# A decoder trunk on one core: convolution taps through PSUM, and the spatial branch's scale and offset behind its product

## The reference, cut to what is computed

```python
def conv_sgu_mixer(x, w_in, conv_w, conv_b, conv_ln_g, conv_ln_b,
                   sgu_ln_g, sgu_ln_b, w_spatial, b_spatial, w_out):
    h = x @ w_in                                   # 1024 -> 2048
    a_val, a_gate, z = h[..., :512], h[..., 512:1024], h[..., 1024:]
    a = a_val * jax.nn.sigmoid(a_gate)
    a = causal_depthwise_conv(a, conv_w) + conv_b  # 31 taps, 512 channels
    a = jax.nn.silu(layer_norm(a, conv_ln_g, conv_ln_b))
    z = jax.nn.gelu(z, approximate=False)
    u, v = z[..., :512], z[..., 512:]
    v = layer_norm(v, sgu_ln_g, sgu_ln_b).reshape(B, 4, 128, 8, 64)
    sv = jnp.einsum('hts,bnshc->bnthc', w_spatial * causal, v) + b_spatial.T[None, None, :, :, None]
    g = u * sv.reshape(B, S, 512)
    return jnp.concatenate([a, g], axis=-1) @ w_out
```

## Time and profile before

| | us |
|---|---|
| median of 3 runs | 1517.16 |
| lowest and highest | 1514.57, 1518.96 |
| the profiled execution, its own time | 1517.05 |
| its span, first to last instruction | 1515.2 |
| PE busy (matmul) | 1420.8, 94% of the span |
| DVE busy | 582.7, 38% |
| ACT busy | 494.0, 33% |
| POOL busy | 656.6, 43% |
| mean granted TensorE clock | 0.971 of full |

### The profile page before, as it was taken

One profiled execution on the slowest core, in us unless ns is written; L12 is line 12 of the kernel. 1 busy time (PEld: TensorE's weight loads), 2 busy tenths in 40 slices (PEclk: granted clock), 3 DMA queues, 4 the chain that ended last, 5 costly groups with the idle time before them and its releaser, 6 DMA issues.

```text
span 1515.2 us, 17072 instructions
## 1 busy us (share of the span) xinstructions
PE 1420.8 (94%) x6631; PEld 1194.2 (79%) x6631; DVE 582.7 (38%) x761; ACT 494.0 (33%) x741; POOL 656.6 (43%) x297
## 2 busy tenths in 40 slices
PE   8981699999999998899999999999998999999997
PEld 7760478888888886788889888889878888888885
DVE  4999754111114004667643566643243111110004
ACT  4442354222222124233333333342343222222112
POOL 4982345444444445333344233334244444444442
PEclk9995699999999999899999999999999999999999
DMA  9220123333332322223232222233122333333221
GB/s 266 73 84 0 61 65 98 97 97 97 97 127 97 97 87 67 69 87 96 84 97 84 70 84 83 80 95 104 42 70 86 95 98 96 97 125 97 97 70 56
DMA packets 175551, 135.27 MB, mean 89 GB/s; under 512 B 4317, under 2 KB 157673, under 8 KB 175496
## 3 DMA queue, kind: packets, MB, share of 16 engines
q1 hardware_dynamic: 175496, 134.50, 29.6%
HBM read 132.39 MB, written 2.10 MB: 89 GB/s over the span
## 4 chain that ended last, share of the span: by engine, by line
PE 83%; DVE 12%; ACT 2%; SPq 1%; issue 1%; POOL 0%; DMA 0%; DVEq 0%
PE pq L540 11%; PE pq L542 11%; PE pq L541 11%; DVE acc L1326 7%; PE ps L540 5%; PE ps L541 5%; PE ps L542 5%; PE pq L562 3%; PE pq L563 3%; PE pq L564 3%; PE ps L564 3%; PE ps L562 3%; PE ps L563 3%; PE pq L844 3%; PE pq L846 2%; PE pq L845 2%
## 5 line engine op out<-in xcount | busy, mean ns | idle before, releaser
L474 POOL TENSOR_TENSOR w_lo<-w_stage,w_hi 128x1024 fp32r<-128x1024 f32 x236 | 573.1, 2433 | 766.0 <-ACT w_hi L934 765.8
L540 PE MATMUL pq<-xt_hi,w_hi 128*128 128x512 f32 (+1 forms) x888 | 339.8, 383 | 8.4 <-DVE xt_lo L1223 5.7
L541 PE MATMUL pq<-xt_lo,w_hi 128*128 128x512 f32 (+1 forms) x888 | 336.3, 379 | 0.0
L542 PE MATMUL pq<-xt_hi,w_lo 128*128 128x512 f32 (+1 forms) x888 | 336.1, 379 | 0.0
L934 ACT ACTIVATE w_hi<-w_stage 128x1024 fp32r<-128x1024 f32 x236 | 245.9, 1053 | 269.0 <-PE ps L564 191.9
L540 PEld LDWEIGHTS pq<-xt_hi,w_hi 128*128 128x128 f32 x888 | 169.5, 191 | 40.3 <-DVE xt_lo L1223 6.4
L542 PEld LDWEIGHTS pq<-xt_hi,w_lo 128*128 128x128 f32 x888 | 169.5, 191 | 30.8
L541 PEld LDWEIGHTS pq<-xt_lo,w_hi 128*128 128x128 f32 x888 | 169.6, 191 | 29.7
L1491 DVE TENSOR_TENSOR hidden<-ps,hidden 128x512 f32<-128x512 f32 x44 | 30.4, 692 | 371.0 <-PE ps L542 371.0
L540 PE MATMUL ps<-xt_hi,w_hi 128*128 128x512 f32 (+1 forms) x368 | 139.9, 380 | 0.0
L541 PE MATMUL ps<-xt_lo,w_hi 128*128 128x512 f32 (+1 forms) x368 | 139.8, 380 | 0.0
(11 more groups left out here) (229 smaller groups left out, 2017.5 us busy)
## 6 DMA issues: line engine op xcount, KB each, us to landing
w_stage<-in_od_w_qkv_dram SPq DMA_DIRECT2D x72, 512.0 KB, 3.8
w_stage<-in_ffn_w_gate_dram SPq DMA_DIRECT2D x44, 512.0 KB, 3.8
w_stage<-in_ffn_w_up_dram SPq DMA_DIRECT2D x44, 512.0 KB, 3.8
w_stage<-in_ffn_w_down_dram SPq DMA_DIRECT2D x44, 512.0 KB, 3.3
w_stage<-in_ev_w_in_dram SPq DMA_DIRECT2D x16, 512.0 KB, 6.3
w_stage<-in_ev_w_out_dram SPq DMA_DIRECT2D x8, 512.0 KB, 3.3
w_stage<-in_od_w_out_dram SPq DMA_DIRECT2D x8, 512.0 KB, 3.3
x_res<-in_x_dram SPq DMA_DIRECT2D x4, 512.0 KB, 6.4
```

The costliest lines, as they stand in the source:

```text
L474: pool.tensor_tensor(w_lo[slab % RING][:, :], w_stage[slab % RING][:, :], w_hi[slab % RING][:, :].bitcast(F32), ALU.subtract).then_inc(w_l ...
L540: pe.matmul(ps[bank][:, at], hi[:, k, :], xt_hi[:, k, at], start=(k == 0), stop=False)
L541: pe.matmul(ps[bank][:, at], hi[:, k, :], xt_lo[:, k, at], start=False, stop=False)
L542: last = pe.matmul(ps[bank][:, at], lo[:, k, :], xt_hi[:, k, at], start=False, stop=(k == KD - 1))
```

## The change

- Of the taps, DVE now has 10 of chunk 0 and 26 of chunk 1, so 98 in all, and ACT with POOL 26, two behind each of slabs 5 to 17.
- DVE's running sums lie in PSUM, bank 6 for chunks 0 and 2, bank 7 for chunks 1 and 3; only a chunk's last DVE tap writes `acc`.
- The spatial product is taken over the value norm without its gain and offset. The gain multiplies behind the product, in the gating instruction. The offset becomes part of `b_sp`: PE sums the masked spatial weights with ones (`sum_spatial`, 8 small matmuls behind slab 3), DVE scales the four offset columns and folds them in with four instructions of 128 x 128. The two value-norm passes on DVE are replaced by one small instruction there and four ACT instructions of 128 x 512.
- The v tiles lie in banks 4, 5, 0, 1 and u in 2, 3, 0, 1, with the waits that this needs. The mean over channels goes to bank 2 and behind the first three spatial pairs.
- The taps are interleaved otherwise: after gate 3 come 24 taps, the four statistics together, 8 taps, the small scale instructions, and the last 32.
- SP: gain and offset are rows of `par_rows` (20 rows instead of 12 turned by PE), the two broadcasts `sgu_g` and `sgu_b` go, `b_sp` comes in two transfers instead of eight, slab 4 is loaded ahead of the spatial weights, the constant table `cst` behind them, and slabs 5 to 7 ahead of the norm's parameters.

The diff, cut:

```diff
-        dve_taps = (8, 22)
+        dve_taps = (10, 26)
         pool_taps = [(c, w) for c in range(2) for w in range(dve_taps[c], CONV_WIDTH)]
         chunk_taps = [CONV_WIDTH - n for n in dve_taps]
-        after_slab = {5: 3, 6: 3, 7: 3, 8: 3, 9: 3, 10: 3, 11: 3, 12: 2, 13: 2, 14: 2, 15: 5}
+        after_slab = dict.fromkeys(range(5, 18), 2)
+        v_banks = (4, 5, 0, 1)
+        u_banks = (2, 3, 0, 1)
+        CONV_B, CONV_G, CONV_O, SGU_G, SGU_B = (CC * CONV_WIDTH + n * CC for n in range(5))
...
-            sp.dma_start(cst[:, :], const_in).then_inc(cst_loaded, 16)
             sp.dma_start(par_rows[0:CONV_WIDTH, 0:CONV_CH], ev_conv_w[0]).then_inc(par_loaded, 16)
-            for n, src in enumerate((ev_conv_b, ev_conv_ln_g, ev_conv_ln_b)):
+            for n, src in enumerate((ev_conv_b, ev_conv_ln_g, ev_conv_ln_b, ev_sgu_ln_g, ev_sgu_ln_b)):
                 sp.dma_start(par_rows[4 * n:4 * n + 4, CONV_CH:CONV_CH + P],
                              src[0].rearrange("(c p) -> c p", p=P)).then_inc(par_loaded, 16)
+            load(RING)
             sp.dma_start(wsp_raw[:, :, :], ev_w_spatial[0].rearrange("h t s -> t h s")).then_inc(wsp_loaded, 16)
-            sp.dma_start(sgu_g[:, :], ev_sgu_ln_g.partition_broadcast(P)).then_inc(sgu_loaded, 16)
-            sp.dma_start(sgu_b[:, :], ev_sgu_ln_b.partition_broadcast(P)).then_inc(sgu_loaded, 16)
-            for h in range(SGU_GROUPS):
-                half = (h % 2) * GROUP_CH
-                sp.dma_start(b_sp[half:half + GROUP_CH, h // 2, :],
-                             ev_b_spatial[0, h:h + 1, :].partition_broadcast(GROUP_CH)).then_inc(sgu_loaded, 16)
+            sp.dma_start(cst[:, :], const_in).then_inc(cst_loaded, 16)
+            load(RING + 1)
+            for half in range(2):
+                rows = ev_b_spatial[0].rearrange("(c two) t -> two c t", two=2)[half:half + 1]
+                sp.dma_start(b_sp[half * GROUP_CH:(half + 1) * GROUP_CH, :, :], rows.broadcast_to([GROUP_CH, CC, P])
+                             ).then_inc(sgu_loaded, 16)
+            for slab in range(RING + 2, RING + 4):
+                load(slab)
             load_ln(0, 0, 0)
-            for slab in range(RING, S_UP0):
+            for slab in range(RING + 4, S_UP0):
...
+            def sum_spatial():
+
+                pe.wait_ge(ones_set, 1)
+                pe.wait_ge(wsp_set, 2)
+                for h in range(SGU_GROUPS):
+                    half = (h % 2) * GROUP_CH
+                    last = pe.matmul(ps[5][half:half + GROUP_CH, h // 2 * P:(h // 2 + 1) * P], ones[:, 0:GROUP_CH],
+                                     wsp_t[:, h, :], start=True, stop=True)
+                last.then_inc(offset_summed, 1)
 
             pe.wait_ge(xt_set, 2 * TILES)
 
@@ -612,15 +628,19 @@
                     columns(slab + j, 2 * (c % 2) + j, (2 if c + j == 0 else 0, TILES)).then_inc(w_used, 1)
                 if c == 0:
                     turn_parameters()
+                if c == 1:
+                    sum_spatial()
...
-            pe.wait_ge(wsp_set, 2)
+            pe.wait_ge(offset_set, 1)
             for s in range(4):
                 slab = S_IN + 8 + s
                 slab_ready(slab)
                 for i in range(TILES):
+                    if s == 0 and i == 2:
+                        pe.wait_ge(a_set, 3)
                     for k in range(2):
-                        last = tokens(slab, 512 * k, 512, 4 + i, xt_hi[:, 2 * s + k, :], xt_lo[:, 2 * s + k, :],
+                        last = tokens(slab, 512 * k, 512, v_banks[i], xt_hi[:, 2 * s + k, :], xt_lo[:, 2 * s + k, :],
...
-                if c % 2 == 0:
-                    pe.wait_ge(a_set, 3 + c // 2)
-                columns(slab, c).then_inc(w_used, 1)
-
-            pe.wait_ge(ones_set, 1)
-            pe.wait_ge(v_gelu, TILES)
-            for c, (which, count) in enumerate(((tap_added, chunk_taps[0]), (tap_added, len(pool_taps)),
-                                                (acc_set, 1), (acc_set, 2))):
-                pe.wait_ge(which, count)
-                last = pe.matmul(ps[7][:, :], ones[:, :], acc[:, c, :], start=(c == 0), stop=(c == CC - 1))
-            last.then_inc(mean_done, 1)
+                if c == 0:
+                    pe.wait_ge(a_set, 4)
+                if c >= 2:
+                    pe.wait_ge(v_gelu, c + 1)
+                columns(slab, u_banks[c]).then_inc(w_used, 1)
 
             def spatial(pair):
                 for n in range(TILES):
@@ -651,8 +665,18 @@
                 last.then_inc(sv_done, 1)
 
             pe.wait_ge(v_set, TILES)
+            pe.wait_ge(sum_begun, 2)
             for pair in range(CC - 1):
+                if pair == CC - 2:
+                    pe.wait_ge(acc_set, 1)
                 spatial(pair)
+            for c, (which, count) in enumerate(((tap_added, chunk_taps[0]), (tap_added, len(pool_taps)),
+                                                (acc_set, 1), (acc_set, 2))):
+                pe.wait_ge(which, count)
+                if c == 0:
+                    pe.wait_ge(u_set, 1)
+                last = pe.matmul(ps[2][:, :], ones[:, :], acc[:, c, :], start=(c == 0), stop=(c == CC - 1))
+            last.then_inc(mean_done, 1)
...
             act.wait_ge(v_var, TILES)
             act.activation(std[:, 0:TILES], mean_var[:, :, 1], ACT.Sqrt, bias=eps[:, 0:1]).then_inc(v_std, 1)
             multiply_taps(15)
+            act.wait_ge(v_scale, 1)
+            for i in range(TILES):
+                act.activation(v_tok[:, i, :], v_tok[:, i, :], ACT.Identity, bias=shift[:, i:i + 1],
+                               scale=rstd[:, i:i + 1]).then_inc(v_set, 1)
             for c in range(CC):
                 act.wait_ge(w_used, S_IN + 12 + c + 1)
-                act.activation(u_t[:, c, :], ps[c][:, :], ACT.Gelu).then_inc(u_set, 1)
-                split_high(16 + c)
+                act.activation(u_t[:, c, :], ps[u_banks[c]][:, :], ACT.Gelu).then_inc(u_set, 1)
+                split_and_taps(16 + c)
...
+                    part = ps[6 + c % 2][:, :]
+                    last = w == (dve_taps[c] if c < 2 else CONV_WIDTH) - 1
                     if w == 0:
-                        ins = dve.tensor_scalar(acc[:, c, :], src, weight, bias, ALU.mult, ALU.add)
+                        ins = dve.tensor_scalar(part, src, weight, bias, ALU.mult, ALU.add)
                     else:
                         link.wait(self_tap[c])
-                        ins = dve.scalar_tensor_tensor(out=acc[:, c, :], in0=src, scalar=weight, in1=acc[:, c, :],
-                                                       op0=ALU.mult, op1=ALU.add)
-                    if c < 2 and w == dve_taps[c] - 1:
-                        ins.then_inc(sum_begun, 1)
-                    elif w == CONV_WIDTH - 1:
-                        ins.then_inc(acc_set, 1)
+                        ins = dve.scalar_tensor_tensor(out=acc[:, c, :] if last else part, in0=src, scalar=weight,
+                                                       in1=part, op0=ALU.mult, op1=ALU.add)
+                    if last:
+                        ins.then_inc(sum_begun if c < 2 else acc_set, 1)
...
+            dve.wait_ge(wsp_set, 2)
+            taps(*((0, w) for w in range(6)))
             gate_in(1)
             dve.wait_ge(a_set, 2)
-            ahead = 8
-            taps(*((1, w) for w in range(dve_taps[1] - ahead)))
+            taps(*(step for w in range(4) for step in ((0, 6 + w), (1, w))))
+            taps(*((1, 4 + w) for w in range(6)))
             gate_in(2)
+            dve.wait_ge(offset_summed, 1)
+            dve.wait_ge(sgu_loaded, 16 * 2)
+            offsets = slice(SGU_B, SGU_B + CC)
+            link.mark(dve.tensor_scalar(par[:, offsets], par[:, offsets], float(CONV_CH), None, ALU.mult))
+            link.wait()
+            for c in range(CC):
+                ins = dve.scalar_tensor_tensor(out=b_sp[:, c, :], in0=ps[5][:, c * P:(c + 1) * P],
+                                               scalar=par[:, SGU_B + c:SGU_B + c + 1], in1=b_sp[:, c, :],
+                                               op0=ALU.mult, op1=ALU.add)
+            ins.then_inc(offset_set, 1)
             dve.wait_ge(a_set, 3)
-            taps(*(step for w in range(ahead) for step in ((1, dve_taps[1] - ahead + w), (2, w))))
+            taps(*(step for w in range(7) for step in ((1, 10 + w), (2, w))))
             gate_in(3)
             dve.wait_ge(a_set, 4)
-            rest = [(2, w) for w in range(ahead, CONV_WIDTH)] + [(3, w) for w in range(CONV_WIDTH)]
-            rest.sort(key=lambda step: step[1] - (ahead if step[0] == 2 else 0))
-            before, between = 42, 1
+            taps(*(step for w in range(9) for step in ((1, 17 + w), (2, 7 + w))))
+            rest = [(2, w) for w in range(16, CONV_WIDTH)] + [(3, w) for w in range(CONV_WIDTH)]
+            rest.sort(key=lambda step: step[1] - (16 if step[0] == 2 else 0))
+            before, after = 6, 8
             taps(*rest[:before])
```

(27 more changed lines are left out.)

27 lines of the change are left out of this document (12 added, 15 removed).

## The result

The changed kernel takes **1461.67 us** (median of 4 runs, 1461.3 to 1468.96) against 1516.76 for the kernel before, measured beside it. The ratio is 0.9653, 95% interval 0.9631 to 0.9674: 3.5% faster. The forecast was 1466. The profiled execution took 1462.03 against 1517.05, so 55.0 less where the sum said 51.2. One of the four executions stands apart, at 1468.96; the other three lie within 0.8 us.

A forecast was written before the change was run, and what follows sets the result against it. DVE's queue of taps, stretched by POOL, was taken to set the output projection's start. Last tap 47.1 us earlier plus a dropped 4.1 wait gave 51.2 off 1517.05: 1466 us, own range 1460 to 1472, 1458 to 1480 with rivals 1 and 4.

The forecast's parts named there:

- The taps: DVE's convolution taps with sums in PSUM: median about 0.74 us, hardly any over 1, not stretched by POOL.
- Rival 1: DVE taps through PSUM are 0.1 to 0.3 us dearer, adding 4 to 12; taken at 0.2, 1474 us; chance 0.13.
- rival 2: POOL still holds DVE's taps up whatever the operand; only 4.1 us is gained, about 1512 us; chance 0.05.
- rival 3: One PSUM bank serves a tap's read and write in turn, 1.38 us a tap; slower, 1526 us; chance 0.05.
- rival 4: DVE's end moves but something else ends last, POOL's last tap or u's gelus; 1474 us; chance 0.05.
- Start: Input projection: changed loads cost nothing, table lands at 31, PE starts slab 4 at 38.35 after 8 more small matmuls.
- POOL's pace: POOL takes 5.18 us a slab, under PE's 5.49, so PE never waits and ends slab 15 at 104.2.
- DVE's wait for the gelus: Ahead of the statistics: DVE's 24 taps end at 77.7, then it waits 8.6 us for v's first gelu at 86.3.
- The tail: DVE from the statistics, ending at 89.5, through 40 taps: last tap ends at 118.7, 47.1 us earlier than before.
- Behind the last tap: Gating follows the last tap at once, saving DVE's 4.14 us wait for PE; other engines finish 8 us or more ahead.
- The sum: 47.1 us from the earlier last tap plus 4.1 from the dropped wait: 51.2 off 1517.05, giving 1466 us.
- so does everything after: From the output projection to the end the same work stands as before, so no gain or loss was counted there.

The follow-up runs named there:

- loads_old: Changed kernel with SyncE issuing the table and parameters in the old order, ahead of slab 4; 1464.79 us, ratio 0.9675 to the kernel before.
- dve_norm: Changed kernel with the value norm's scale and offset back on DVE in eight passes, nothing folded behind the spatial product; 1478.93 us, ratio 0.9739 to before.
- mean_first: Changed kernel with the four mean matmuls ahead of the first spatial pairs again on PE; 1469.97 us, ratio 0.9708 to the kernel before.
- sbuf_sums: Changed kernel with the running sums of the DVE taps back in SBUF, all else kept; 1510.05 us, ratio 0.9946 to the kernel before.

## Why the prediction was right, point by point

The mechanism and the likeliest case held, and the time lay 4.3 us under the forecast, inside its range.

- **The taps.** Forecast: a median near 0.74, hardly any over 1. Measured: 0.750, the longest 0.759. The first tap of a chunk, which the forecast didn't set apart, takes 0.81 into PSUM. Rival 1 (dearer by 0.1 to 0.3), rival 2 (POOL still holds DVE) and rival 3 (1.38) fell, and so did rival 4: POOL's splits stay at 2.42. The Trainium skill's 62 cycles more for a PSUM operand (page "VectorE: DVE Perf Modes", section on the TRN2 errata) would be, by an estimate from it, 0.065 a tap. The rows show 0.750 against 0.739, so 0.01, and the taps start as close together as before.
- **Start.** Forecast: slab 4 starts on PE at 38.35. It started 0.6 earlier, at 37.76, after the spatial weights' transposes began at 24.81 instead of 25.68. The order of the loads isn't the reason: loads_old has these transposes at 25.04, and 0.54 of the difference is there in PE's first matmul already (5.25 against 5.79). The table, put at 31, had landed at 24.7 (issued at 15.22, 9.5 on its way).
- **POOL's pace.** Forecast 5.18 a slab, measured 5.07 (splits at 50.77 and 55.84). PE never waited, and ended the projection at 103.3 against a forecast of 104.2.
- **DVE's wait for the gelus.** Forecast: one wait, 8.6. Measured: 3.72 ahead of gate 2 and 4.46 ahead of the statistics, 8.2 in all. I had forgotten that gate 2 waits for a sigmoid and this for slab 5, so the 24 taps ended at 80.4 and not at 77.7. It cost nothing, as the gelus were still the later of the two, by 4.46. That was luck: the forecast had not weighed this wait. The first was done at 84.8, not 86.3, by POOL's pace and the earlier start.
- **The tail.** Forecast 118.7 for the last tap, measured 116.9; from the end of the statistics (89.5 forecast, 88.0 measured) it took 28.8 where 29.2 were forecast.
- **Behind the last tap.** The 4.14 wait went as forecast, and the restart came at 121.18 against 123. The slack of the rest was as forecast: u's first gelu at 97.95, POOL's last tap ending at 109.6.
- **The sum.** 51.2 was forecast, 55.0 came. 2.1 of the difference is the earlier restart (53.3 where 51.2 were forecast), most of it the 1.5 by which the gelus came sooner. The other part is the step "so does everything after": norm 2's pair at L1298 fell from 5.41 to 3.35, which is 2.06, without anything in the change touching it. No term of the sum stood for it. I had read the earlier trace rows as an average and taken the stretch for fixed.
- **The parts.** The sum gave 14.5 to the value norm's passes (dve_norm: 15.0) and 4.1 to PE's order (mean_first: 5.1). The remainder was put down to taps that no longer wait for POOL, against six taps more. sbuf_sums gives 43.6 to the operand's place. Together these are 63.7, more than 53.3. They need not add up, since each part is priced here with the others in place; how the parts overlap was not measured.

## What to carry to other kernels

Where VectorE and GpSimd work side by side, look at each VectorE instruction for two operands in SBUF, and at one like the first tap here, which reads one and writes SBUF. Moving the running sum to PSUM took the hold away from both; it cost 0.01 us a tap, and 0.27 on the first. Where a gain up front is not in the time, cut both spans at the same events and compare the stretches: here it was given back 60 and 970 us later, by the same conflict in code that nobody had edited. A wait added to an engine that is early can be the cure.
